# Loading whole expert matrices, with slots of their own for the odd pairs' gates, in a three-layer transformer kernel

## The reference

```python
def grouped_moe(h, router_w, router_bias, w_gate, w_up, w_down):
    ...
    for e in range(N_EXPERTS):
        he = jax.nn.silu(t @ w_gate[e]) * (t @ w_up[e])
        out = out + gates[:, e:e + 1] * (he @ w_down[e])
    return out.reshape(B, S, D)
```

## Time and profile before

| | us |
|---|---|
| median of three runs | 1598.32 (1597.41 to 1599.08) |
| the profiled execution | 1605.66 |
| its span, first to last instruction | 1603.9 |
| TensorE busy | 1514.8 (94%) |
| VectorE busy | 599.2 (37%) |
| ScalarE busy | 417.7 (26%) |
| mean TensorE clock granted | 0.973 |

### The profile page before, as it was taken

The page is one execution under the profiler, slowest core; times in us unless marked ns, Lnnn a source line. Parts: engine busy times, 40 slices in busy tenths (PEclk is TensorE's granted clock), DMA queues, the critical chain, the costliest instruction groups (busy, mean ns, idle before and its releaser), DMA issues.

```text
span 1603.9 us, 24144 instructions
## 1 busy us (share of the span) xinstructions
PE 1514.8 (94%) x9543; PEld 836.0 (52%) x9543; DVE 599.2 (37%) x1383; ACT 417.7 (26%) x956; POOL 62.6 (4%) x79
## 2 busy tenths in 40 slices
PE   7999999999999999999998999889999999999997
PEld 3665664444446647544443866557554444434433
DVE  3453552322354263533323165433433322332232
ACT  1142331212132433412111433353212121121121
POOL 0000010000010001100000044001000000000000
PEclk9999989999999999999999999799999999999999
DMA  9998779999999778799999300612799999999995
GB/s 353 351 337 299 299 294 423 422 422 422 422 384 342 281 296 320 314 422 422 422 422 408 120 1 1 255 60 93 288 421 422 422 422 422 422 422 423 422 422 241
DMA packets 122474, 535.35 MB, mean 334 GB/s; under 512 B 11023, under 2 KB 14953, under 8 KB 73266
## 3 DMA queue, kind: packets, MB, share of 16 engines
q1 hardware_dynamic: 122002, 534.40, 83.1%
q10 hardware_dynamic: 416, 0.17, 0.0%
HBM read 533.48 MB, written 1.06 MB: 333 GB/s over the span
## 4 chain that ended last, share of the span: by engine, by line
PE 66%; DMA 26%; DVE 3%; ACT 2%; issue 1%; SPq 1%; POOL 0%; DVEq 0%; POOLq 0%; ACTq 0%
PE pair L1047 17%; DMA ring<-in_w_dram 16%; DMA ring<-in_moe_w_gate_dram 8%; PE bank L769 7%; PE pair L1071 4%; PE bank L1071 3%; PE pair L1149 3%; PE bank L666 3%; PE bank L1033 2%; PE bank L863 2%; PE bank L1085 2%; PE bank L776 2%; PE pair L745 2%; DMA ring<-in_a_w_qkv_dram 1%; PE bank L1149 1%; PE bank L1024 1%
## 5 line engine op out<-in xcount | busy, mean ns | idle before, releaser
L1047 PE MATMUL pair<-ring,arena 128*64 128x512 f32 x2048 | 455.5, 595 | 30.4 <-DMA ring<-in_w_dram 21.6
L1047 PEld LDWEIGHTS pair<-ring,arena 128*64 128x64 f32 x2048 | 140.8, 137 | 313.3 <-issue 271.1
L2432 DVE SCALAR_TENSOR_TENSOR xT<-bank,mod,xT 128x256 f32<-128x256 f32 x180 | 75.9, 477 | 171.5 <-PE bank L1085 171.5
L1071 PE MATMUL pair<-ring,arena 128*64 128x512 f32 x512 | 127.1, 619 | 2.1 <-ACT arena L1772 2.1
L1071 PE MATMUL bank<-ring,arena 128*64 128x512 f32 x512 | 121.1, 593 | 0.0
L769 PE MATMUL bank<-hh,ring 128*128 128x256 f32 x512 | 117.3, 386 | 2.0 <-DMA ring<-in_a_w_qkv_dram 2.0
L769 PEld LDWEIGHTS bank<-hh,ring 128*128 128x128 f32 x512 | 96.8, 192 | 24.2 <-issue 8.6
L2418 DVE SCALAR_TENSOR_TENSOR arena<-sq,arena,pair 128x512 f32<-128x512 f32 x32 | 35.6, 1113 | 175.6 <-PE pair L1047 175.6
L1772 ACT ACTIVATE arena<-pair 128x512 f32<-128x512 f32 x32 | 19.1, 597 | 266.7 <-PE pair L1109 266.7
L2426 DVE TENSOR_TENSOR arena<-pair,arena 128x512 f32<-128x512 f32 x32 | 22.1, 692 | 159.9 <-ACT arena L1778 159.9
L1033 PE MATMUL bank<-arena,hh 128*128 128x128 bf16 x928 | 81.0, 219 | 0.2 <-DVE arena L2296 0.2
(11 more groups left out here) (419 smaller groups left out, 1891.3 us busy)
## 6 DMA issues: line engine op xcount, KB each, us to landing
ring<-in_w_dram SPq DMA_DIRECT2D x192, 1024.0 KB, 23.1
ring<-in_moe_w_gate_dram SPq DMA_DIRECT2D x64, 1024.0 KB, 17.4
ring<-in_moe_w_up_dram SPq DMA_DIRECT2D x64, 1024.0 KB, 17.9
ring<-in_moe_w_down_dram SPq DMA_DIRECT2D x64, 1024.0 KB, 18.4
ring<-in_ada_w_dram SPq DMA_DIRECT2D x24, 2048.0 KB, 17.2
ring<-in_w_mod_dram SPq DMA_DIRECT2D x12, 2048.0 KB, 12.3
ring<-in_a_w_qkv_dram SPq DMA_DIRECT2D x6, 2048.0 KB, 20.3
ring<-in_b_w_qkv_dram SPq DMA_DIRECT2D x6, 2048.0 KB, 19.9
```

Source lines behind the costliest of these rows:

```text
L1047: last = mm(b[2 + m][half(a), :], x_sel[:, k, half(a)], R8[moe_slot(l, a, m)][:, k, :], start=(k == 0), stop=(k == KT - 1))
L1071: last = mm(b[5 + n][half(a), :], hidT[:, f, half(a)], R4[moe_slot(l, a, 2)][:, f, n * 512:(n + 1) * 512], start=(f == 0), stop=(f == FT - 1))
L2432: last = stt(xT[:, k, :], (sums_last if last_pair else sums)[r][:, k % 2 * S:(k % 2 + 1) * S], mod[:, l, G2 + k:G2 + k + 1], xT[:, k, :], ...
```

## The change

1. Each expert matrix is one load of 2 MiB, a run of 16 KiB in a partition, with one semaphore, and TensorE waits for the whole matrix and releases the whole matrix. `down` takes all four blocks of its first 512 output columns and then all four of the second, where it took two blocks of each in turn; its releases are two where there were three.
2. In stages one and three the gates of odd pairs (1, 3, ...) have two slots of their own (`spare_slots`): one in `arena`, one in `hh`. The gates of pair 1 are issued behind those of pair 0's downs, and after that the gates of pair i+2 are issued when pair i's gates are consumed, ahead of the ups and downs of pair i+1. For this, `tok_part` lies in `sq` and in `arena` in these stages. Stage two keeps six slots and the order of before.
3. TensorE's loop does two pairs a turn, since the slot of a gate now depends on the pair's parity; the last two pairs stand behind the loop. VectorE writes one more small value for the loop's bound. The loops of ScalarE and VectorE stay over single pairs.
4. In stages one and three, in the last pair but one, the gate products of the last pair stand ahead of the down products (`gate_first`).
5. `after_experts` may issue into the two gate slots of the ring one pair earlier in stages one and three.

The core of the diff:

```diff
+        by_part = lambda a: a.bitcast(BF16).rearrange("p (n t k c) -> p n t k c", n=a.shape[1] // D, t=TT, c=P)
...
-        lowest = arena[:, 12420:13444].bitcast(BF16).rearrange("p (t k c) -> p t k c", t=TT, c=P)
-        def tok_part(n, t):
-            return lowest[:, t] if n == 2 else halves[:, 2 * n + t]
+        lowest, top, lower = by_part(arena[:, 12420:13444]), by_part(sq[:, 512:1536]), by_part(arena[:, 12544:14592])
+        def tok_part(l, n, t):
+            if l == 1:
+                return lowest[:, 0, t] if n == 2 else halves[:, 2 * n + t]
+            return top[:, 0, t] if n == 0 else lower[:, n - 1, t]
...
-            MOE[l]["done"] = ((MOE[l]["gate_ps"], 2), (MOE[l]["up_ps"], 2), (MOE[l]["down_ps"], 3))
-            MOE[l]["full"] = [[sem(f"{n}_full{h}_{l}") for h in range(2)] for n in ("gate", "up", "down")]
+            MOE[l]["done"] = (MOE[l]["gate_ps"], MOE[l]["up_ps"], MOE[l]["down_ps"])
+            MOE[l]["full"] = [[sem(f"{n}_full{h}_{l}") for h in range(parts)] for n, parts in (("gate", 1), ("up", 1), ("down", 1))]
+            MOE[l]["full_odd"] = [sem(f"odd_gate_full_{l}")] if l != 1 else None
...
+        R8 = [ring[s][:, :].rearrange("p (k n) -> p k n", k=KT) for s in range(NSLOT)]
+        R4 = [ring[s][:, :].rearrange("p (k n) -> p k n", k=FT) for s in range(NSLOT)]
+        spare_slots = (view(8448, KT, CHUNK), hh[:, :, :])
+        DOWN_STEPS = 2
+        def expert_slot(l, a, m, is_odd):
+            s = moe_slot(l, a, m)
+            if m == 0 and l != 1 and is_odd:
+                return spare_slots[a]
+            return (R4 if m == 2 else R8)[s]
...
-            def expert(l, a, m, e, h):
-                s = moe_slot(l, a, m)
-                w = (GATE_W, UP_W, DOWN_W)[m][l]
-                n = (FT if m == 2 else KT) // 2
-                src = w[bass.ds(e, 1)].rearrange("a (p k) n -> p (a k) n", p=P)
-                dst = ring[s][:, :].rearrange("p (k n) -> p k n", k=2 * n)
-                sp.dma_start(dst[:, h * n:(h + 1) * n, :], src[:, h * n:(h + 1) * n, :]).then_inc(MOE[l]["full"][m][h], 16)
-            def pair_loads(l, i, before):
-                for m in range(3):
-                    done, steps = MOE[l]["done"][m]
-                    for h in range(2):
-                        sp.wait_ge(done, before * steps - (steps - 1 if h == 0 else 0))
-                        for a in range(2):
-                            expert(l, a, m, 2 * i + a, h)
+            def expert(l, a, m, i, is_odd):
+                dst = expert_slot(l, a, m, is_odd)
+                n = (FT if m == 2 else KT)
+                src = (GATE_W, UP_W, DOWN_W)[m][l][bass.ds(2 * i + a, 1)].rearrange("a (p k) n -> p (a k) n", p=P)
+                parts = MOE[l]["full_odd"] if m == 0 and l != 1 and is_odd else MOE[l]["full"][m]
+                n //= len(parts)
+                for h, part in enumerate(parts):
+                    sp.dma_start(dst[:, h * n:(h + 1) * n, :], src[:, h * n:(h + 1) * n, :]).then_inc(part, 16)
+            def both(l, m, i, is_odd=0):
+                for a in range(2):
+                    expert(l, a, m, i, is_odd)
+            def following(l, i, is_odd, gates):
+                gate, up, down = MOE[l]["done"]
+                if gates and l != 1:
+                    sp.wait_ge(gate, i + 1)
+                    both(l, 0, i + 2, is_odd)
+                if l == 1:
+                    sp.wait_ge(gate, i + 1)
+                    both(l, 0, i + 1)
+                sp.wait_ge(up, i + 1)
+                both(l, 1, i + 1)
+                sp.wait_ge(down, DOWN_STEPS * i + DOWN_STEPS)
+                both(l, 2, i + 1)
+            def further(l, r, i, is_odd):
+                gate, up, down = MOE[l]["done"]
+                at = r * (EXPERTS[l] // 2) + i + EXPERTS[l] // 2
+                sp.wait_ge(gate, at if l == 1 else at - 1)
+                both(l, 0, i, is_odd)
+                sp.wait_ge(up, at)
+                both(l, 1, i)
+                sp.wait_ge(down, DOWN_STEPS * at)
+                both(l, 2, i)
...
                             sp.wait_ge(update_ps, 4)
-                        for h in range(2):
-                            expert(l, a, m, a, h)
-                with sp.Fori(1, E // 2) as i:
-                    pair_loads(l, i, i)
+                        expert(l, a, m, 0, 0)
+                if l != 1:
+                    sp.wait_ge(out_proj, 16 * l + 16)
+                    both(l, 0, 1, 1)
+                with sp.Fori(0, E // 4 - 1) as j:
+                    following(l, 2 * j, 0, True)
+                    following(l, 2 * j + 1, 1, True)
+                following(l, E // 2 - 2, 0, False)
                 sp.wait_ge(n_ready, turn(n_ready))
...
                     with sp.Fori(0, more) as r:
-                        with sp.Fori(0, E // 2) as i:
-                            pair_loads(l, i, r * (E // 2) + i + E // 2)
+                        with sp.Fori(0, E // 4) as j:
+                            further(l, r, 2 * j, 0)
+                            further(l, r, 2 * j + 1, 1)
                 more_rounds[l] = more
...
                 for k in range(NSLOT):
-                    done, steps = MOE[l]["done"][k // 2]
-                    sp.wait_ge(done, more_rounds[l] * (EXPERTS[l] // 2 * steps) + EXPERTS[l] // 2 * steps)
+                    steps = (1, 1, DOWN_STEPS)[k // 2]
+                    early = 1 if k < 2 and l != 1 else 0
+                    sp.wait_ge(MOE[l]["done"][k // 2],
+                               more_rounds[l] * (EXPERTS[l] // 2 * steps) + (EXPERTS[l] // 2 * steps - early))
                     fenced.add(n + k - NSLOT)
...
-                                last = mm(b[part][:, cols(k % 4)], tok_part(n, t)[:, k, :], pick_part[:, t, :],
+                                last = mm(b[part][:, cols(k % 4)], tok_part(l, n, t)[:, k, :], pick_part[:, t, :],
...
-                def project(i, m):
+                def project(j, is_odd, m):
+                    i = 2 * j + is_odd
...
-                        if k % 4 == 0:
-                            pe.wait_ge(M["full"][m][k // 4], 32 * i + 32)
+                        if k == 0 and (m == 1 or l == 1):
+                            pe.wait_ge(M["full"][m][0], 64 * j + 32 * is_odd + 32)
+                        elif k == 0:
+                            pe.wait_ge(M["full_odd"][0] if is_odd else M["full"][0][0], 32 * j + 32)
...
-                            last = mm(b[2 + m][half(a), :], x_sel[:, k, half(a)], R8[moe_slot(l, a, m)][:, k, :],
+                            last = mm(b[2 + m][half(a), :], x_sel[:, k, half(a)], expert_slot(l, a, m, is_odd)[:, k, :],
...
-                        if k % 4 == 3:
-                            last.then_inc(M["up_ps" if m else "gate_ps"], 1)
+                    last.then_inc(M["up_ps" if m else "gate_ps"], 1)
...
-                    for h in range(2):
-                        pe.wait_ge(M["full"][2][h], 32 * i + 32)
-                        for n in range(2):
-                            for f in (2 * h, 2 * h + 1):
-                                for a in range(2):
-                                    last = mm(b[5 + n][half(a), :], hidT[:, f, half(a)],
-                                              R4[moe_slot(l, a, 2)][:, f, n * 512:(n + 1) * 512],
-                                              start=(f == 0), stop=(f == FT - 1))
-                            if h + n >= 1:
-                                last.then_inc(M["down_ps"], 1)
+                    pe.wait_ge(M["full"][2][0], 32 * i + 32)
+                    for n in range(2):
+                        for f in range(FT):
+                            for a in range(2):
+                                last = mm(b[5 + n][half(a), :], hidT[:, f, half(a)],
+                                          R4[moe_slot(l, a, 2)][:, f, n * 512:(n + 1) * 512],
+                                          start=(f == 0), stop=(f == FT - 1))
+                        last.then_inc(M["down_ps"], 1)
...
-                m = pe.value_load(nit[0:1, 0:1], min_val=1, max_val=ROUNDS * EXPERTS[l] // 2 - 1)
-                project(0, 0)
+                m = pe.value_load(nit[0:1, 2:3], min_val=1, max_val=ROUNDS * EXPERTS[l] // 4 - 1)
+                project(0, 0, 0)
...
-                def pair_of(i, last_pair):
-                    project(i, 1)
+                def pair_of(j, is_odd, last_pair, gate_first=False):
+                    i = 2 * j + is_odd
+                    project(j, is_odd, 1)
...
                     pe.wait_ge(M["hidT_ready"], i + 1)
+                    if gate_first:
+                        project(j + is_odd, 1 - is_odd, 0)
                     down(i)
...
                     else:
-                        project(i + 1, 0)
+                        if not gate_first:
+                            project(j + is_odd, 1 - is_odd, 0)
                         combine(i, sums)
...
-                with pe.Fori(0, m) as i:
-                    pair_of(i, False)
```

(19 more changed lines are left out.)

8 lines of the change are left out of this document (3 added, 5 removed).

## The result

| | before | changed |
|---|---|---|
| median of 16 runs | 1599.28 us | 1603.97 us |
| profiled execution | 1605.66 us | 1604.05 us |
| its span | 1603.9 us | 1602.3 us |

The ratio of changed to before is 1.0024, with a 95% interval of 1.0015 to 1.0034: 3.8 us slower, 2.4 to 5.4 (the medians of the table differ by 4.7). The direction is the forecast one, and the time lies inside the range of 1597 to 1620 us. The size is less than half of the 10.7 us forecast.

The account below looks back on a forecast made before the run. Transfers (29.82 us a pair) were taken to bound the expert stages over TensorE (27.2 us). Stages +9.2 and clock +1.5 gave +10.7 us on the median 1598.3: 1609.0 us, range 1597 to 1620.

Parts of the forecast that it names:

- What bounds the kernel, and u: Expert stages: transfers set the pace; u, the transfer of two matrices, goes from 9.94 to 9.80 us.
- the rival with a unit of 9.64 us: Expert loads: larger fixed cost per run, so longer runs make the change win, 1595 us; chance 0.10.
- the one in which long runs gain nothing: Expert loads: 16 KiB runs no faster than 8 KiB, 1618.4 to 1621.4 us; chance 0.18.
- The release half a gate later: Start of each stage: whole-matrix release delays every later load by 3.4 us; stage two also pays at its end.
- The two unequal counts of units: Transfers up to the last bound wait: 17 in stage one, 41 in stage three; +4.2 and +0.9 us.
- The slots for the odd gates: Stages one and three: two units fewer (19.9 us) before the last bound wait, then TensorE's full 27.2 us pair.
- The rival of the filled gap: Stage ends: a stage ends with its last byte, 6.5 us earlier in stages one and three; 1581 us, chance 0.07.
- The gate ahead of the down product: Last pairs of stages one and three: copy wait 0.9 plus combine idle 1.8, 2.7 us more on TensorE's path.
- the rival of the fetched body: TensorE's doubled loop: body fetched each turn, 1 to 5 us on top, 1611 to 1614 us; within the forecast's 0.60.
- What follows the up products isn't touched: After each stage's last up products: no change in time, if the last downs have landed.
- the term of 1.5 us for the clock: Last pair but one, stage one or three: half clock after a 2.2 us wait costs 1.5 us, bounds 0 to 3.0.
- the sum's 9.2: The three expert stages, up to the last pair's up products: together +9.2 us at 9.80 us per unit.

Follow-up runs that it names:

- e3_short_runs: The changed kernel with each matrix loaded in two halves (runs of 8 KiB); 1618.13 us, ratio to before 1.0122.
- e9_first_pair_halves: Changed kernel without part 4, old down order, pair 0's gates, ups, downs released and reloaded by halves, stage two's last gates in halves; 1590.11 us, ratio to before 0.9948.
- e1_whole: The kernel before with part 1 alone (whole matrices, six slots, old load order) in all stages; 1603.92 us, ratio to before 1.0024.
- e2_gate_behind: The changed kernel without part 4, last pair's gate products behind the down products again; 1598.31 us, ratio to before 0.9999.
- e8_first_half: Changed kernel without part 4, first gates behind pair 0's release loaded in halves, also stage two's last gates; 1595.54 us, ratio to before 0.9982.
- the second look: The kernel before, unchanged, run for a second profiled execution; 1596.85 us.
- e4: Changed kernel without part 4, last pair's gates in stages one and three loaded behind the previous pair's ups and downs; 1598.40 us, ratio to before 0.9995.
- e6: The kernel before with the gather's 48 matmuls added on TensorE in each stage's last pair, results unread; 1596.24 us, ratio to before 0.9993.

## Why the prediction was right or wrong

**What bounds the kernel, and u.** Right. 9.79 us for 9.80, from a straight line through runs of 2 and 8 KiB. The rate is 428 GB/s, so the rival with a unit of 9.64 us is out, as is the one in which long runs gain nothing (e3_short_runs shows what that would cost). The Trainium skill (DMA: Bandwidth & Descriptors, section "Where 436 GB/s comes from") has its ceiling at 435.2 GB/s; 428 GB/s stays below.

**The release half a gate later.** Right: +3.9 us in stage two, 4.1 summed, and e9_first_pair_halves, which takes it back in the first pair, gains what was summed in stages one and three (3.5 and 3.3 us for 3.4). The two unequal counts of units are right too: stages one and three are longer by 4.1 and 0.5 us, for 4.2 and 0.9.

**The slots for the odd gates.** Right. The gap in the queue shrank from 12 us to 5. Busy time by stretch, changed kernel, against the earlier trace rows:

```profile
1124.00:1130.00 6.00, 6.00 (x35) 6.00 (x35) 3.65 (x22) 1.24 (x4) 0.00 (x0) 0.62 1.01 429
1130.00:1139.00 9.00, 9.00 (x59) 4.06 (x59) 7.68 (x16) 3.01 (x7) 0.00 (x0) 1.00 0.46 197
```

But the last bound wait moved ahead to the ups of the last pair but one, and TensorE's full pair behind it ate most of the gain. Two kernels show what is left: e1_whole has whole matrices and no slots, e2_gate_behind has the slots and not part 4. With u = 9.79 us the prediction's terms give 2u - 27.2 + 10.2 = 2.6 us between them; stages one and three differ by 2.2 and 2.4 us. Part 4 then costs as much again. The rival of the filled gap, 1581 us, is out.

**The gate ahead of the down product.** Right: 2.3 and 2.5 us for 2.7. The idle piece in the combine is 1.40 us for 1.8, and the wait for the copy of `x_sel` ahead of the gate products 0.75 us for 0.9. The last downs were not waited for in stages one and three.

**Parts with one answer.** The doubled loop body is not fetched at each turn: queue q8 in 1150 to 1550 us of the changed kernel has two blocks, where the earlier trace rows has one.

```profile
q8 instruction: 2, 0.03, 0.0%
```

These 400 us hold six turns and more, and one turn (1249.94 to 1308.69 us) has 771 recorded instructions of TensorE (matmuls and weight loads), so the rival of the fetched body is out. By the Trainium skill (Runtime: NRT & Kernel Launch, section "Instruction fetch mechanics"), TensorE buffers 2048 instructions; the trace agrees with that.

**The clock.** Here the prediction failed. The step is "What follows the up products isn't touched", together with the term of 1.5 us for the clock, which was mis-sized, in sign as well. The rows behind "the clock stays at 1.00" end at 1574 us, ahead of the last pair's down products. In the first profile these ran at half clock for 3.4 us in each stage (0.83 over ten us). In the changed kernel that is gone from stages one and three, which gives back 1.5 + 1.9 = 3.4 us, 3.2 of it in the down products themselves. The loss that I had put on one of the pairs 6 and 14 did not fall there: the half clock appeared in the stages (at 377.6, 793.8, 1309, 1367, 1456 and 1514 us), as the single wait of 2.0 us suggested, but elsewhere than in these pairs, where it costs nothing since it eats the next wait. Where it falls is not decided by this sum: in e8_first_half it fell on both, 1.7 and 1.6 us, and in e3_short_runs on pair 6. So the term was not wrong in kind; that this kernel paid nothing of it is luck, as far as the runs show. Forecast +1.5, measured -3.4: 4.9 of the 5.6 us between 10.7 us and the 5.1 us of the profiles. The other 0.7 is the sum's 9.2 for 8.5. The runs themselves say 3.8 us, with 5.1 inside their interval.

**The base.** Adding to the median of the runs and not to the profiled execution was right, as the second look shows; against the profile the forecast would have been 7 us higher. The expected span of 1614.6 us did just that, and was 12 us over the measured 1602.3.

What stays open is what decides the clock of the last pair. The half clock is there in 5 of 6 stages in the two profiles of the kernel before. In the seven profiles of kernels with the change or a part of it and without added matmuls (runs by their first two signs) it is there in 4 of 21: in stage two of the changed kernel, e1 (again) and e4, in stage three of e3, and in none of e2, e8 and e9. e6 shows that filling the idle removes it. But the same idle pieces can be followed by either clock. The first down products of the last pair in stage two, the kernel before in its first and in its second profile, behind 1.26 us of idle ahead of the transposes in both:

```profile
866.08 3.57 PE L1071 MATMUL pair<-ring,arena 128*64 128x512 f32 x8 [0.69 <-ACT arena L1772]
```

```profile
864.50 1.94 PE L1071 MATMUL pair<-ring,arena 128*64 128x512 f32 x8 [0.69 <-ACT arena L1772]
```

The new order inside `down` is not the reason that it is rarer: e9 has the old order and no half clock in a last pair. Part 4 is not either: e1 and e2 lack it. What precedes by 15 us differs (in e1 one wait of 1.9 us instead of two shorter ones, in e2 a full pair without a wait); no run separates this.

## What to carry to other kernels

When a stage is bound by a queue of loads, write the place of each load in the queue, and find the last one that is waited for: behind it the compute engine's own pace counts, and a gain ahead of an earlier wait is worth only the slack that is left there. Buffers that fill a gap at the start of a stage are paid back at its end if what they load early stands in the queue ahead of what is waited for: here two units, 19.6 us, shrank to 2.2 and 2.4 us. Coarser loads raise the rate (runs of 16 KiB instead of 8: 1.5%), but coarser releases delay the first reload of every buffer in turn; keep the releases of the first pass fine, all of them (gates alone moved the last wait by 1.9 to 2.0 us, all three by 3.2 to 3.5), and take the long runs after that. And where a forecast says that a part isn't touched, look at its granted clock as well: here it was the largest error.

## What the runs showed of the hardware

Loads into 128 partitions flowed at 387 to 391 GB/s with runs of 2 KiB (loads of 2 MiB), 422 with 8 KiB (1 MiB) and 428 with 16 KiB (2 MiB). By an estimate from these rates, with 16 engines, they lie on one line with some 9 ns fixed per run. A single wait of 2.0 us on TensorE was followed by half clock in some pairs (8.81 us for the up products instead of 7.09) and not in others: in stage three of the changed kernel in 4 of 7. In the last pair half clock for 3.4 us made the down products 1.7 us longer (8.8 us instead of 7.1). From the last ups of stage two to stage three the two profiles of the kernel before differ by 7.5 us, 6.0 of them in the third attention, with its clock (0.82 and 0.89), which is more than this change moves.
